# GLA levels of a hybrid decoder block: two token tiles in one matmul, queries and keys scaled in place

## What is computed

```python
# b = running sum over tokens of the log decay (all <= 0), per key channel d
attn[i, j] = sum_d q[i, d] * k[j, d] * exp(b[i, d] - b[j, d])     for j <= i, else 0
o[i]       = sum_j attn[i, j] * v[j]
```

## Times and profile of the kernel before

| | |
|---|---|
| three runs, us | 1609.13, 1610.9, 1612.62 (median 1610.9) |
| the profiled execution's own time | 1611.82 us |
| its span in the profile | 1610.0 us, mean granted TensorE clock 0.995 |
| TensorE matmul busy | 1590.1 us, 99% |
| VectorE busy | 1134.1 us, 70% |
| ScalarE busy | 818.7 us, 51% |
| GpSimd busy | 7.3 us |

### The profile page before, as it was taken

How to read it: one execution, slowest core, us unless ns; L and a number is a source line. 1 busy time by engine, 2 the same in 40 slices (tenths; PEclk the granted TensorE clock), 3 DMA queues, 4 the chain that set the end, 5 groups by cost and what they waited for, 6 DMA issues and landing times.

```text
span 1610.0 us, 29554 instructions
## 1 busy us (share of the span) xinstructions
PE 1590.1 (99%) x11788; PEld 1496.4 (93%) x11788; DVE 1134.1 (70%) x1331; ACT 818.7 (51%) x1068; POOL 7.3 (0%) x11
## 2 busy tenths in 40 slices
PE   7999999999999999999999999999999999999998
PEld 7999999879999999999888999999999999888886
DVE  5888767886977786877766677777777665644444
ACT  5567776656544643434446545455554544434332
POOL 0000000001000000000000000000000000000000
PEclk9999999999999999999999999999999999999999
DMA  9999988873458887877864777777777656555553
GB/s 370 355 326 345 324 268 256 284 251 128 128 195 293 284 293 242 290 268 261 325 225 129 242 238 236 236 246 236 252 236 221 200 184 209 185 196 194 184 195 143
DMA packets 190648, 389.41 MB, mean 242 GB/s; under 512 B 18386, under 2 KB 31058, under 8 KB 189794
## 3 DMA queue, kind: packets, MB, share of 16 engines
q1 hardware_dynamic: 185666, 370.33, 68.8%
q10 hardware_dynamic: 4898, 17.90, 3.3%
HBM read 386.09 MB, written 2.10 MB: 241 GB/s over the span
## 4 chain that ended last, share of the span: by engine, by line
PE 94%; DVE 3%; ACT 2%; issue 1%; DMA 0%; DVEq 0%; ACTq 0%
PE ps L579 20%; PE ps L581 20%; PE ps L583 20%; PE ps L606 8%; PE ps L608 8%; PE ps L607 8%; PE ps L783 2%; PE ps L531 1%; DVE w_lo L1385 1%; PE ps L722 1%; DMA x_tok<-in_x 0%; PE ps L690 0%; PE ps L798 0%; PE ps L721 0%; PE ps L656 0%
## 5 line engine op out<-in xcount | busy, mean ns | idle before, releaser
L1385 DVE TENSOR_TENSOR w_lo<-raw,w_hi 128x1024 fp32r<-128x1024 f32 x530 | 625.7, 1221 | 422.4 <-ACT w_hi L969 421.6
L969 ACT ACTIVATE w_hi<-raw 128x1024 fp32r<-128x1024 f32 x530 | 533.0, 1052 | 654.5 <-PE ps L583 426.4
L579 PE MATMUL ps<-h2t,w_hi 128*128 128x256 f32 x1408 | 389.8, 277 | 0.6 <-DVE h2t L1815 0.6
L581 PE MATMUL ps<-h2t,w_hi 128*128 128x256 f32 x1408 | 388.7, 276 | 0.0
L583 PE MATMUL ps<-h2t,w_lo 128*128 128x256 f32 x1408 | 388.7, 276 | 0.0
L579 PE MATMUL ps<-ht,w_hi 128*128 128x256 f32 x1104 | 310.5, 281 | 0.0
L581 PE MATMUL ps<-ht,w_hi 128*128 128x256 f32 x1104 | 306.8, 278 | 0.0
L583 PE MATMUL ps<-ht,w_lo 128*128 128x256 f32 x1104 | 306.7, 278 | 0.0
L579 PEld LDWEIGHTS ps<-h2t,w_hi 128*128 128x128 f32 x1408 | 264.3, 188 | 0.8 <-issue 0.8
L581 PEld LDWEIGHTS ps<-h2t,w_hi 128*128 128x128 f32 x1408 | 264.4, 188 | 0.0
L583 PEld LDWEIGHTS ps<-h2t,w_lo 128*128 128x128 f32 x1408 | 264.3, 188 | 0.0
(11 more groups left out here) (279 smaller groups left out, 2032.8 us busy)
## 6 DMA issues: line engine op xcount, KB each, us to landing
raw<-in_w_ffn_up SPq DMA_DIRECT2D x176, 512.0 KB, 4.5
raw<-in_w_in SPq DMA_DIRECT2D x168, 512.0 KB, 5.2
ada<-in_w_ada SPq DMA_DIRECT2D x148, 512.0 KB, 6.5
raw<-in_w_ffn_down SPq DMA_DIRECT2D x88, 512.0 KB, 4.0
raw<-in_w_branch_b SPq DMA_DIRECT2D x32, 512.0 KB, 5.4
raw<-in_w_mix_out SPq DMA_DIRECT2D x32, 512.0 KB, 5.0
ada<-in_w_ada ACTq DMA_DIRECT2D x32, 512.0 KB, 4.1
raw<-in_w_branch_a SPq DMA_DIRECT2D x16, 512.0 KB, 5.3
```

Source lines behind the costliest of these rows:

```text
L579: mm(o, w_hi[:, s, k, cols], moving[:, kt, 0], start=opens, stop=False, skip_group_check=True)
L581: mm(o, w_hi[:, s, k, cols], moving[:, kt, 1], start=False, stop=False, skip_group_check=True)
L969: A(w_hi[:, slot], raw[:, slot], ACT.Copy).then_inc(hi_done, 1)
L1385: V.tensor_tensor(w_lo[:, slot], raw[:, slot], w_hi[:, slot].bitcast(F32), ALU.subtract)\
```

## The change

Queries and keys are no longer computed from untouched `q_gla`, `k_gla` and a fresh exponential. They are scaled in place from level to level: one exponential of all of `dec` at level 1, after which each level multiplies the second halves of `q_gla` by the product of the decays of the first half-block, the first halves of `k_gla` by that of the second (a broadcast column), and shrinks `dec` by one multiplication. `scan`, `suf` and the later exponentials go.

ScalarE copies the operands of a level into `qk[lv % 2]`. The first 128 columns hold the keys of tile 0 in first-half places and the queries of tile 1 in second-half places; the other 128 columns the keys of tile 1 and the queries of tile 0. One product of the two gives, in one 128x128 result per head, tile 0's level (keys x queries) in one triangle and tile 1's level, transposed, in the other. A mask that is symmetric selects both into `attn_c`. Behind level 8 four transposes bring the second triangle to `attn1`.

```diff
@@ level_masks
-        out.append((i // (2 * h) == j // (2 * h)) & (j % (2 * h) < h) & (i % (2 * h) >= h))
+        below = (i // (2 * h) == j // (2 * h)) & (j % (2 * h) < h) & (i % (2 * h) >= h)
+        out.append(below | below.T)
+    out.append(j < i)
@@ buffers (masks and masks_i grow from LEVELS - 1 = 8 to LEVELS = 9 slabs)
-        qk = at(B + 120, "qk", [P, 8, S], F32, 8)
+        qk = [at(B + 120, "qk0", [P, 8, S], F32, 8), at(B + 104, "qk1", [P, 8, S], F32, 8)]
+        attn_c = at(B + 96, "attn_c", [P, GH, P], F32, 2)
+        def odd_halves(v, h):
+            return v.rearrange("p d (b s h) -> p d b s h", s=2, h=h)[:, :, :, 1]
+        def scaled_at(lv):
+            return 3 * lv - 2
@@ TensorE
             def level(lv):
-                if lv:
-                    pe.wait_ge(qk_ready, lv)
-                    pe.wait_ge(level_taken, lv)
...
+                elif lv < LEVELS - 1:
+                    pe.wait_ge(qk_ready, lv)
+                    pe.wait_ge(level_taken, max(1, lv - 1))
+                else:
+                    pe.wait_ge(scaled, scaled_at(lv))
+                    pe.wait_ge(level_taken, lv - 1)
+                for t in range(NT if lv == 0 else 1):
                     for hd in range(GH):
                         for i in range(2):
                             d = 2 * hd + i
...
+                            elif lv < LEVELS - 1:
+                                bank, lhs, rhs = 6 + lv % 2, qk[lv % 2][:, d, 0:P], qk[lv % 2][:, d, P:S]
                             else:
+                                bank, lhs, rhs = 6, k_gla[:, d, 0:P], q_gla[:, d, P:S]
+                            ins = mm(ps[:, bank, hd * P:(hd + 1) * P], lhs, rhs, start=i == 0, stop=i == 1)
                 ins.then_inc(level_ready, 1)
+            def flip_second():
+                pe.wait_ge(level_taken, LEVELS - 1)
+                for hd in range(GH):
+                    ins = nc.tensor.transpose(ps[:, 7, hd * P:(hd + 1) * P], attn_c[:, hd, :], ident[:])
+                ins.then_inc(flip_ready, 1)
             def gla_out(pr):
                 if pr < 2:
-                    pe.wait_ge(level_taken, LEVELS)
+                    pe.wait_ge(level_taken, LEVELS + 1)
...
                 if 1 <= k - GLA - 1 < LEVELS:
                     level(k - GLA - 1)
+                if k == GLA + LEVELS:
+                    flip_second()
@@ ScalarE
-            def decays(lv):
+            def decays():
+                act.wait_ge(pre_ready, 1)
+                for part in (1, 0):
+                    A(halves(dec, 1)[part], halves(pre, 1)[part], ACT.Exp, scale=1.0 / TAU).then_inc(dec_ready, 1)
+            def operands(lv):
                 h = 1 << (lv - 1)
-                act.wait_ge(scan_ready, lv - 1)
-                act.wait_ge(qk_ready, lv - 1)
-                A(d1, halves(pre, h)[1], ACT.Exp, scale=1.0 / TAU)
-                A(d0, halves(suf, h)[0], ACT.Exp, scale=1.0 / TAU).then_inc(dec_ready, 1)
+                both = qk[lv % 2]
+                act.wait_ge(scaled, scaled_at(lv))
+                if lv > 2:
+                    act.wait_ge(level_ready, lv - 1)
+                A(halves(both, h)[0], halves(k_gla, h)[0], ACT.Copy)
+                A(odd_halves(both[:, :, 0:P], h), odd_halves(q_gla[:, :, P:S], h), ACT.Copy)
+                A(odd_halves(both[:, :, P:S], h), odd_halves(q_gla[:, :, 0:P], h), ACT.Copy).then_inc(qk_ready, 1)
...
                 if k == GLA + 1:
-                    decays(1)
+                    decays()
+                    operands(1)
...
-                    if 2 <= k - GLA <= LEVELS - 1:
-                        decays(k - GLA)
+                    if 2 <= k - GLA < LEVELS - 1:
+                        operands(k - GLA)
                     if last and kind not in ("ba", "bb"):
                         if (kind, g) == ("ga", 0):
-                            act.wait_ge(qk_ready, LEVELS - 1)
+                            act.wait_ge(level_ready, LEVELS)
@@ VectorE (products and scan are removed)
+            def first_scale(part):
+                dve.wait_ge(level_ready, 1)
+                dve.wait_ge(dec_ready, 2 - part)
+                q = halves(q_gla, 1)[part]
+                V.tensor_tensor(q, q, halves(dec, 1)[part], ALU.mult).then_inc(scaled, 1)
+            def widen(lv):
+                h = 1 << (lv - 2)
+                dve.wait_ge(qk_ready, lv - 1)
+                dve.wait_ge(scaled, 3 * lv - 4)
+                first, second = (v[:, :, 0:1] for v in halves(dec, h))
+                q, k = halves(q_gla, h)[1], halves(k_gla, h)[0]
+                V.tensor_tensor(q, q, spread(first, q), ALU.mult).then_inc(scaled, 1)
+                V.tensor_tensor(k, k, spread(second, k), ALU.mult).then_inc(scaled, 1)
+                if lv < LEVELS - 1:
+                    dve.wait_ge(scaled, scaled_at(lv))
+                    V.tensor_tensor(first, first, second, ALU.mult).then_inc(scaled, 1)
             def select(lv):
...
                 elif lv < LEVELS - 1:
-                    for b, dst in ((6, attn0[:, :, 0:P]), (7, attn1)):
-                        for hd in range(GH):
-                            src = ps[:, b, hd * P // 2:(hd + 1) * P // 2].rearrange("p (b h) -> p b h", h=h)
-                            ins = V.copy_predicated(second(dst[:, hd]), m, src)
+                    dve.wait_ge(attn_zero, 3)
+                    V.copy_predicated(attn_c[:], m, by_head(6 + lv % 2)).then_inc(level_taken, 1)
                 else:
                     V.tensor_copy(attn0[:, :, P:S], by_head(6)).then_inc(level_taken, 1)
+                    dve.wait_ge(flip_ready, 1)
+                    V.copy_predicated(attn1[:], m, by_head(7))
+                    V.copy_predicated(attn0[:, :, 0:P], m, attn_c[:]).then_inc(level_taken, 1)
                 dve.wait_ge(level_taken, lv + 1)
...
                 if k == GLA + 1:
-                    products(1)
-                    scan(1)
+                    first_scale(1)
...
                     select(0)
-                    V.tensor_copy(halves(qk, 1)[0], halves(k_gla, 1)[0])
                     log_decay()
                 if 1 <= k - GLA - 1 < LEVELS:
                     select(k - GLA - 1)
+                if k == GLA + 1:
+                    first_scale(0)
                 if 2 <= k - GLA < LEVELS:
-                    products(k - GLA)
-                    if k - GLA < LEVELS - 1:
-                        scan(k - GLA)
+                    widen(k - GLA)
@@ GpSimd
-            pool.wait_ge(pre_ready, 1)
-            nc.gpsimd.memset(suf[:], 0.0).then_inc(decay_ready, 1)
+            pool.wait_ge(dec_ready, 2)
+            nc.gpsimd.memset(attn_c[:], 0.0).then_inc(attn_zero, 1)
```

More of the change, by code:

```diff
@@ L187, in build @@
         ones = sb("ones", [P, P], F32)
-        masks = sb("masks", [P, LEVELS - 1, P], U8)
+        masks = sb("masks", [P, LEVELS, P], U8)
         cos_t = sb("cos_t", [P, S], F32)
@@ L236, in build @@
         red = at(B + 37, "red", [P, 2, S], F32, 2)
-        masks_i = at(B + 39, "masks_i", [P, LEVELS - 1, P], I32, 4)
+        masks_i = at(B + 39, "masks_i", [P, LEVELS, P], I32, 5)
         lat = at(B + 116, "lat", [P, 6, S], F32, 6)
@@ L310, in build @@
                                                     sem("xt_copied"))
-        recip_x, attn_zero, suffix_ready = sem("recip_x"), sem("attn_zero"), sem("suffix_ready")
+        recip_x, attn_zero, flip_ready = sem("recip_x"), sem("attn_zero"), sem("flip_ready")
         pre_ready, og_folded, half_used, first_used = sem("pre_ready"), sem("og_folded"), sem("half_used"), sem("first_used")
@@ L321, in build @@
                                                           sem("ctx_hi"), sem("ctx_lo"))
[L322 to L325, removed]
+        gate_psum, gate_pre, gate_soft = sem("gate_psum"), sem("gate_pre"), sem("gate_soft")
+        dec_ready, qk_ready, scaled, level_ready, level_taken = (
+            sem("dec_ready"), sem("qk_ready"), sem("scaled"), sem("level_ready"), sem("level_taken"))
         og_psum, og_copied, og_squared, og_summed, og_rms, og_silu, og_gated, og_hi, og_lo = (
@@ L759, in level @@
             def level(lv):
-                if lv:
-                    pe.wait_ge(qk_ready, lv)
-                    pe.wait_ge(level_taken, lv)
-                else:
+                if lv == 0:
                     pe.wait_ge(gate_pre, 8)
@@ L767, in level @@
                     pe.wait_ge(tile_empty, START[PAIRS[MLA][0]][0] + 2)
-                n_q = P if lv in (0, LEVELS - 1) else P // 2
-                for t in range(NT if lv < LEVELS - 1 else 1):
+                elif lv < LEVELS - 1:
[5 more added lines that the diff above has]
+                for t in range(NT if lv == 0 else 1):
@@ L770, in level @@
                     for hd in range(GH):
-                        o = ps[:, 6 + t, hd * n_q:(hd + 1) * n_q]
                         for i in range(2):
                             d = 2 * hd + i
-                            keys = slice(t * P, (t + 1) * P)
```

(43 more changed lines are left out.)

## The result

The changed kernel takes 1652.1 us (median), the kernel before 1611.8 beside it: ratio 1.0251, 95% interval 1.0234 to 1.0269. It is 40 us slower. The forecast was 1610.3, between 1605.0 and 1615.5, so the result lies far outside.

The account below looks back on a forecast made before the run. TensorE, busy 99% of the span, was taken to bound the kernel. Saved level matmuls -12.2, a fourth transpose +0.4 and waits +11.2 gave -0.6 us: 1610.3 us on the median, range 1605 to 1615.5.

Parts of the forecast that it names:

- edits costed at nothing: GLA stage's start and end, decay product, ninth mask slab, zeroing, buffer guards: all covered by other work, 0 us.
- slower rivals: GLA stage: clock falls in waits (1619 us, 11%), levels cost as before (1612.4, 2%), copies near upper bound (1614 to 1616, 5%).
- The loop: GLA stage, ScalarE and VectorE queues wait on each other: 8.65 us an index, 10.62 or 9.60 at some, TensorE needs 7.46.
- the walk: GLA stage, followed level by level from level 1 at 399.09 us: pair 64 ends at 470.41, before at 471.03.
- TensorE's own work: GLA stage: new levels 1.78 us instead of 3.52, saving 12.2; four transposes 0.44; balance -11.7 us.
- unwaiting rival: GLA stage: TensorE doesn't wait, as both other engines have room in sum; -11.7 us, 1599.2 us; chance 8%.
- The waits: GLA stage, levels 2 to 7: TensorE waits for operand copies six times, 1.2 to 3.2 us each, 11.2 in sum.
- clock rival: GLA stage: TensorE's clock falls in its waits; 1619 us if every second index is slow, +26 if all six; 11%.
- the slack that was worked out for it: GLA stage: TensorE has 1.2 us or more against the loop; a slowdown decides only beyond that in an index.
- rule on columns: GLA levels: a 128-column matmul takes twice a 64-column one, so new levels cost as old; +1.5 us, 1612.4; chance 2%.

Follow-up runs that it names:

- E1: The kernel before with an unused tile of 128 bytes a partition behind the masks, against the kernel before: 1652.7 us, ratio 1.0258.
- E5: Changed kernel, buffers at their former addresses, a level's scaling put ahead of VectorE's lo splits, against the kernel before: 1598.9 us, ratio 0.9927.
- E2: Changed kernel with the ninth mask slab in another buffer's unused part, every buffer at its former address, against the kernel before: 1612.4 us, ratio 1.0005.

## Why the prediction was wrong, point by point

**The step that failed** stands among the edits costed at nothing: "The ninth mask slab makes the cast of 686 ns an eighth longer and the load 64 KB larger". Both are so, and both are covered. But the slab's own 128 bytes a partition were not costed. They move every large buffer against the weights, and nearly every row of split products in the kernel then runs at 117.8 ns a product where most ran at 113.4. It cost +42 us (E1: 1652.7 without any other edit). The trace of before held a hint that I passed over: the distance between split products is no constant of the instruction (5.68 / 48 = 118 ns in the GLA stage, 113 in the FFN lines above), although the buffers are the same. It gave no price for another address, so the honest entry was a cost with one open end. My slower rivals all sat in the GLA stage.

**The loop** was right, in length and in kind. One beat of the changed kernel, VectorE and ScalarE:

```profile
420.20 0.74 DVE L1628 COPY_PREDICATED attn_c<-masks,ps 128x512 f32<-128x512 uint8 x1
420.97 1.23 DVE L1608 TENSOR_TENSOR q_gla<-q_gla,dec 128x1024 f32<-128x1024 f32 x1
422.11 1.22 DVE L1609 TENSOR_TENSOR k_gla<-k_gla,dec 128x1024 f32<-128x1024 f32 x1
```

```profile
416.84 2.00 ACT L987 ACTIVATE w_hi<-raw 128x1024 fp32r<-128x1024 f32 x2
423.37 1.06 ACT L1137 ACTIVATE qk<-k_gla 128x1024 f32<-128x1024 f32 x1 [4.53 <-DVE k_gla L1609]
424.33 0.61 ACT L1138 ACTIVATE qk<-q_gla 128x512 f32<-128x512 f32 x1
424.85 0.61 ACT L1139 ACTIVATE qk<-q_gla 128x512 f32<-128x512 f32 x1
425.37 1.99 ACT L987 ACTIVATE w_hi<-raw 128x1024 fp32r<-128x1024 f32 x2
```

From hi splits to hi splits 425.37 - 416.84 = 8.53 us, forecast 8.65; with empties 9.5, forecast 9.60; at index 56 it is 416.84 - 406.15 = 10.69, forecast 10.62. ScalarE's 4.53 us of idle behind its splits are the loop: it waits for VectorE, which waited for it. The stage takes 71.04 us, the walk gave 71.2. E5 shows the loop to be the cause, by taking it apart.

**TensorE's own work**: a new level 1.78 us (2.05 right behind a wait), four transposes 0.44, both as forecast. The unwaiting rival's -11.7 us are E5's -11.8, but it is luck that they agree to 0.1: the rival had pairs of 5.68 us, E5 has most of them at 5.46, and gives some of this back in later rows.

**The waits**: 8.1 us in the list, in five places, the longest 2.8; forecast 11.2 in six, the longest 3.2.

```profile
PE ps L792 <- ACT qk L1139: 8.1, 5, 2.8
```

By level, forecast and found: 1.4 and 1.5, 3.2 and 2.8, 1.2 and none, 2.1 and 1.3, 1.2 and 0.7, 2.1 and 1.8. The largest part of the missing 3.1 us, 1.2 at level 4, is the clock; of the other 1.9 a loop that is 0.1 us shorter than forecast each time explains some. Windows of the changed kernel around it (length, engines, granted clock, DMA):

```profile
424.00:426.40 2.40, 0.88 (x7) 0.89 (x8) 0.47 (x1) 2.40 (x5) 0.00 (x0) 0.99 0.05 19
426.40:429.80 3.40, 3.40 (x18) 3.40 (x17) 3.32 (x4) 0.96 (x2) 0.00 (x0) 0.51 0.26 53
429.80:434.00 4.20, 4.20 (x38) 4.20 (x37) 2.85 (x3) 2.12 (x4) 0.00 (x0) 1.00 0.60 211
```

TensorE worked 0.88 of 2.40 us, then the clock stood at 1.2 GHz for 3.4 us and came back. The next level started without a wait and the loop lost nothing (hi splits at 425.37, the next at 434.91, 9.5 us). The clock rival's mechanism is real, happened once behind a wait of this stage, and cost nothing, by the slack that was worked out for it. The Trainium skill ("TensorE: Matmul & The Clock Gate", "Part 1: The HAM clock gate") has the clock throttled unless activity releases it; the trace agrees, 0.51 behind the wait.

**The rule on columns** (level cost as before): no, 1.78 us. The Trainium skill ("TensorE: Matmul & The Clock Gate", "Back-to-back issue gap"), which the prediction names for this rule, gives the formula for an isolated matmul and says that it under-counts at few columns, where weight loads take part. So the 110 and 111 ns a record don't contradict it; the prediction read the formula too widely.

**Edits at nothing** otherwise: E2, which has them all and the move not, is at 1.0005. Right in sum; no run prices them one by one.

## What to carry to other kernels

Growing a small table moves everything allocated behind it; where TensorE streams products, keep the distance between its two operands' buffers when you edit, or give the new bytes a place that moves nothing, and run the old kernel with a pad before judging the edit. When time appears in lines that nobody edited, compare the distance between starts, not the durations. And an order of queues can hold a loop that sums of busy time don't show: write down one beat through both queues, then take the longest foreign work (here two lo splits) out of it.

## What the runs showed of the hardware that I had not expected

The spacing that prevails among back-to-back split products depends on the distance between the weight buffer and the other operand's: 113.3 ns at moves of 0 and 256 bytes a partition, 120.0 at 64, 117.7 at 128, 118.7 at 192, while the recorded duration of one stays at 276 to 286 ns. Single rows of products depart from it, at 117.8 in the good places and at 113.4 in the one of 128 bytes, and keep their value until they are interrupted. The Trainium skill ("TensorE: Matmul & The Clock Gate", "Step-by-step: what each phase is for") says that loading the next weights doesn't steal read bandwidth from the running matmul, as the two have separate ports. The runs don't bear that out for every placement, as far as spacing goes: with nothing but a pad added, the spacing that prevails is 4 to 7 ns longer than 113. That it is read bandwidth which is lost is not shown.
